# One more gate tile and eight key pages in the chain block; output weights with a second home in a decoder step

## The reference, cut to what matters

```python
oa, s_new, shift_new = rwkv_branch(za, shift0, s0, p)      # recurrent branch, a chain over the tokens
q, k, v, log_f = fox_features(zb, p['f_bias'], p['q_norm'], p['k_norm'])
ob = attend(q, k, v, log_f)                                 # samples: 16 pages of 128 keys and values each
merged = jax.nn.sigmoid(ga) * (oa @ p['proj_a']) + jax.nn.sigmoid(gb) * (ob @ p['proj_b'])
return (merged @ p['w_out']).astype(h.dtype), (k, v, log_f, s_new, shift_new)
```

## Time and profile before

| | |
|---|---|
| median of three runs | 859.84 us (859.52 to 865.72) |
| the profiled execution | 862.67 us, span 861.0 us |
| TensorE busy | 761.1 us, 88% of the span |
| VectorE, ScalarE, GpSimd busy | 382.5, 186.4, 145.3 us |
| mean granted TensorE clock | 0.942 |
| DMA | 220.26 MB, 256 GB/s over the span |
| chain that ended last, by engine | PE 17%, DMA 6%, DVE 1% of the span |

### The profile page before, as it was taken

How to read it: one execution, slowest core, us unless ns; L and a number is a source line. 1 busy time by engine, 2 the same in 40 slices (tenths; PEclk the granted TensorE clock), 3 DMA queues, 4 the chain that set the end, 5 groups by cost and what they waited for, 6 DMA issues and landing times. The chain is left out here.

```text
span 861.0 us, 20782 instructions
## 1 busy us (share of the span) xinstructions
PE 761.1 (88%) x8681; PEld 445.5 (52%) x8681; DVE 382.5 (44%) x722; ACT 186.4 (22%) x433; POOL 145.3 (17%) x294
## 2 busy tenths in 40 slices
PE   5999999998989999768898997889889987899985
PEld 2445666675666667624565664455644425444421
DVE  2222623228963174748666774633552222422213
ACT  2101321216332210031422320223111110111103
POOL 8500120007020020031504343422000000000000
PEclk9999999988999989768899998999989998999997
DMA  8721431211332113459899999988939999999993
GB/s 311 284 86 54 190 117 49 97 53 67 103 85 84 32 55 85 105 163 396 364 352 414 397 397 409 362 313 314 422 153 425 421 425 421 426 420 425 421 412 121
DMA packets 54647, 220.26 MB, mean 256 GB/s; under 512 B 21935, under 2 KB 24026, under 8 KB 30746
## 3 DMA queue, kind: packets, MB, share of 16 engines
q1 hardware_dynamic: 46576, 183.28, 54.5%
q0 software_dynamic: 7328, 35.48, 10.7%
q10 hardware_dynamic: 650, 0.18, 0.1%
HBM read 211.82 MB, written 7.09 MB: 254 GB/s over the span
## 5 line engine op out<-in xcount | busy, mean ns | idle before, releaser
L232 PE MATMUL bank<-arena 128*128 128x320 f32 x256 | 85.0, 469 | 3.1 <-DVEq L2200 1.8
L208 POOL DMA_DIRECT2D arena<-in_cv x116 | 59.9, 516 | 113.1 <-PE bank L1897 80.8
L513 PE MATMUL bank<-arena 128*128 128x512 f32 (+1 forms) x144 | 69.9, 624 | 1.4 <-DMA arena<-in_w_zb 1.4
L2508 PE MATMUL bank<-arena 128*32 128x512 f32 x512 | 65.4, 624 | 3.3 <-DMA arena<-in_w_exp 2.1
L2739 DVE TENSOR_TENSOR arena<-arena,bank 128x512 f32<-128x512 f32 x35 | 24.1, 687 | 97.2 <-PE bank L2478 94.2
L548 PE MATMUL bank<-arena 128*128 128x336 f32 x224 | 66.3, 450 | 0.6 <-ACT arena L429 0.6
L1590 DVE STREAM_TRANSPOSE arena<-arena 128x2048 f32<-128x2048 f32 x28 | 63.1, 2288 | 4.3 <-DMA arena<-in_ck 2.9
L232 PEld LDWEIGHTS bank<-arena 128*128 128x128 f32 x256 | 47.5, 199 | 24.8 <-issue 7.6
L1897 PE MATMUL bank<-arena 128*16 128x128 f32 x1024 | 35.6, 300 | 19.7 <-issue 11.4
L548 PEld LDWEIGHTS bank<-arena 128*128 128x128 f32 x224 | 41.5, 189 | 21.4 <-issue 1.7
L1389 ACT ACTIVATE arena<-bank 128x384 f32<-128x384 f32 (+6 forms) x63 | 25.1, 444 | 108.2 <-PE bank L232 31.9
(11 more groups left out here) (495 smaller groups left out, 1103.4 us busy)
## 6 DMA issues: line engine op xcount, KB each, us to landing
arena<-in_w_exp SPq DMA_DIRECT2D x95, 1024.0 KB, 19.1
arena<-in_ck SPq DMA_DIRECT2D x120, 256.0 KB, 6.6
arena<-in_cv POOLq DMA_DIRECT2D x116, 256.0 KB, 7.6
arena<-in_w_gate SPq DMA_DIRECT2D x8, 1024.0 KB, 4.8
arena<-in_w_za SPq DMA_DIRECT2D x7, 1024.0 KB, 6.9
arena<-in_w_zb SPq DMA_DIRECT2D x6, 1024.0 KB, 15.7
arena<-in_w_proj SPq DMA_DIRECT2D x8, 512.0 KB, 9.9
arena<-in_w_out SPq DMA_DIRECT2D x4, 1024.0 KB, 10.6
```

The lines of the kernel that those rows point to most:

```text
L208: eng.dma_start(tile[n:P:4, :], src[bass.ds(page, 1)].rearrange("a (p j) n -> (a p) (j n)", j=4))\
L232: mm = nc.tensor.matmul(bank[b][:, 0:TM], w[:, k, a, :], xnT[:, k, NMETA:T], start=(k == 0), stop=(k == KT - 1))
L513: mm = nc.tensor.matmul(bank[q % 6][0:n, :], xnT[:, k, i * P:i * P + n], w[:, k % 4, :], start=(k == 0), stop=(k == KT - 1))
L2508: mm = nc.tensor.matmul(bank[2][j * CAP:(j + 1) * CAP, :], xg[:, q % 2, k, j * CAP:(j + 1) * CAP], place[s][:, (k % 4) * 512:(k % 4 + 1) * ...
```

## The change

- `GT_PAIRS` is 15. Passes eight and nine of the chain get a quarter of tile 14 each; its other four matmuls lie among the output products, one behind the 2nd, 5th, 8th and 11th of twelve groups. Its copy follows on ScalarE, its store on SyncE. One tile is left to "cache". Output products use bank 4 in place of 3, the state's transposes bank 5.
- `cd` and `um` move in the arena behind `place[12]`, `xl` into `ar`, so that places 11 and 12 are free during the chain. SyncE loads key tiles 0 and 1 of sample 1 (eight pages, 2 MB) there, behind `rsuf` and ahead of the stores of tiles 12 to 14.
- In "cache" SyncE begins with key tile 2 of sample 1 (GpSimd keeps tile 3, now behind the gate stores), and it stores the state after the first projections. VectorE turns the first key tile before it waits for the variance, the second before the reciprocal.
- The gates are kept as two parts, prompt and samples; each gates load is two DMAs (8 runs of 1024 and of 256 bytes for each partition), and an `a` fill is two multiplies.
- `w_out[2]` is loaded twice: for the fills into `spare` (the prompt part of the gates) once the merge sum is complete, ahead of the keys of sample 7, and later into place 0 for the samples' output. `w_out[0]` and `[1]` come ahead of the keys of sample 6, `w_out[3]` ahead of the second copy of `[2]`.
- Fills are dealt 6, 2, 4, 5, 5, 5, 5 and none ahead of the weighing of sample 7.

```diff
-        GT_PRE, GT_LEVELS, GT_SOLVE, GT_SAMPLES, GT_PAIRS = 6, 9, 11, 12, 14
+        GT_PRE, GT_LEVELS, GT_SOLVE, GT_SAMPLES, GT_PAIRS = 6, 9, 11, 12, 15
...
+                for m in range(2):
+                    load_pages(sp, 11 + m, page_numbers(sp, m, 1), A["ck"])
                 gates_out(GT_SAMPLES, GT_PAIRS)
-                for i in range(2):
-                    sp.wait_ge(S(f"kept_gt{i}"), 16 * (GT_PAIRS // 2))
-                sp.wait_ge(S("w_sp_sb"), 1)
-                for g in range(NPAIR):
-                    sp.dma_start(O["rw_p"][2 * g:2 * g + 2]...).then_inc(S("kept_rw"), 16)
...
-                    if c < 7:
-                        chain_gate(c + 1)
+                    chain_gate(c + 1)
+
+                OUT_BANK = (0, 1, 2, 4)
                 pe.wait_ge(S("w_s"), NCH)
-                pe.wait_ge(S("w_gt_sb"), GT_PAIRS - GT_PRE)
+                pe.wait_ge(S("w_o1_sb"), 1)
...
+                        n = g * NT + j
+                        if n % 3 == 1:
+                            mm = gate_mm(pe, GT_PAIRS - 1, 3, (4 + n // 3,))
+                            if n // 3 == 3:
+                                mm.then_inc(S("w_gt"), 1)
+                pe.wait_ge(S("w_o1_sb"), 2)
...
-        fill_no = [0, 0, 5, 8, 11, 14, 18, 24, 28, len(kinds)]
+        fill_no = [0, 0, 6, 8, 12, 17, 22, 27, len(kinds), len(kinds)]
...
                 def gates_load(a):
-                    sp.dma_start(gates, gates_dram[a]).then_inc(S("gates_in"), 16)
-
-                for m in range(2):
-                    load_pages(sp, key_slot(1, m), page_numbers(sp, m, 1), A["ck"])
+                    sp.dma_start(gates, gates_dram[a, :, :, 0:SEQ]).then_inc(S("gates_in"), 16)
+                    sp.dma_start(gates_s, gates_dram[a, :, :, SEQ:TM]).then_inc(S("gates_in"), 16)
+
+                for n, page in enumerate(page_numbers(sp, 2, 1)):
+                    page_load(sp, place[key_slot(1, 2)], n, A["ck"], page, S("kept_key2"))
                 proj_load(sp, 0, 0)
                 proj_load(sp, 0, 1)
+                for g in range(NPAIR):
+                    sp.dma_start(O["rw_p"][2 * g:2 * g + 2]...).then_inc(S("kept_rw"), 16)
...
                 key_loads(5)
-                key_loads(6)
                 out_load(sp, 0)
                 out_load(sp, 1)
+                key_loads(6)
+                sp.wait_ge(S("m_ready"), ND)
+                sp.dma_start(spare, A["w_out"][2]).then_inc(S("spare_in"), 16)
                 key_loads(7)
                 sp.wait_ge(S("sco_ps"), DB - 1)
+                out_load(sp, 3)
                 out_load(sp, 2)
-                out_load(sp, 3)
...
-                for m in range(2, 4):
-                    pages = page_numbers(pool, m, 1)
-                    for n in range(4):
-                        page_load(nc.gpsimd, place[key_slot(1, m)], n, A["ck"], pages[n], S(f"kept_key{m}"))
+                pages = page_numbers(pool, 3, 1)
+                for i in range(2):
+                    pool.wait_ge(S(f"kept_gt{i}"), 16 * ((GT_PAIRS + 1 - i) // 2))
+                for n in range(4):
+                    page_load(nc.gpsimd, place[key_slot(1, 3)], n, A["ck"], pages[n], S("kept_key3"))
...
                 turn_bias(0)
+                turn_keys(1, 0)
                 dve.wait_ge(S("ov_ps"), 1)
                 TS(ovs, bank[7][:, 0:T], 1.0 / HD, GN_EPS, mult, add).then_inc(S("ov_ready"), 1)
-                turn_keys(1, 0)
+                turn_keys(1, 1)
                 dve.wait_ge(S("ort_ready"), 1)
                 nc.vector.reciprocal(ovs, ovs).then_inc(S("ov_rc"), 1)
-                turn_keys(1, 1)
```

More of the change, by code:

```diff
@@ L1446, in _ @@
                 gate_out(GT_SOLVE, 7)
-                for j in range(GT_SAMPLES, GT_PAIRS):
-                    gate_out(j, 3)
+                gate_out(GT_SAMPLES, 3)
+                gate_out(GT_SAMPLES + 1, 3)
                 act.wait_ge(S("w_or"), NCH)
@@ L1605, in out_load @@
             sp.dma_start(place[s], A["w_out"][c]).then_inc(full[s], 16)
-        gates = xnT.rearrange("p k t -> p (k t)")[:, 0:DM // P * TM].rearrange("p (d t) -> p d t", d=DM // P)
+        gates_all = xnT.rearrange("p k t -> p (k t)")[:, 0:DM // P * TM]
+        gates = gates_all[:, 0:SLOT].rearrange("p (d t) -> p d t", d=DM // P)
+        gates_s = gates_all[:, SLOT:].rearrange("p (d t) -> p d t", d=DM // P)
+        assert DM // P * SEQ == SLOT
+        spare = gates_all[:, 0:SLOT]
         valid = ident.rearrange("p (g c) -> p g c", g=NPAIR)[:, :, 0:2 * DS]
@@ L1683, in proj_fill, with out_full @@
             return full[proj_slot[2 * a + h]], 32 * (1 + (2 * a + h == 3))
+        out_tile = [place[out_slot[0]], place[out_slot[1]], spare, place[out_slot[3]]]
         def out_fill(c):
+            if c == 2:
+                return S("spare_in"), 16
+            return out_full(c)
+        def out_full(c):
             return full[out_slot[c]], (48, 16, kneed(6, 0) + 16, kneed(6, 1) + 16)[c]
@@ L2035, in _ @@
                 pe.wait_ge(S("sb_sb"), 1)
+                pe.wait_ge(*out_full(2))
                 for k in range(KT):
@@ L2238, in fill_out @@
                     if kind == "a":
-                        TT(mT[:, d, :], out[:, 0:TM], gates[:, d, :], mult).then_inc(S("fill_sb"), 1)
+                        ch(TT(mT[:, d, 0:SEQ], out[:, 0:SEQ], gates[:, d, :], mult))
+                        ch(TT(mT[:, d, SEQ:TM], out[:, SEQ:TM], gates_s[:, d, :], mult))
+                        dve.sem_inc(S("fill_sb"), 1)
                     else:
-                        ch(TT(btmp, out[:, 0:SEQ], gates[:, d, 0:SEQ], mult))
+                        ch(TT(btmp, out[:, 0:SEQ], gates[:, d, :], mult))
                         dve.sem_inc(S("fill_sb"), 1)
```

37 lines of the change are left out of this document (22 added, 15 removed).

## The result

| | median us | lowest to highest | runs |
|---|---|---|---|
| before | 862.78 | 859.52 to 867.46 | 4 |
| changed | 882.25 | 879.81 to 887.37 | 4 |

The ratio is 1.0245, 95% interval 1.0199 to 1.0291. The forecast was 849.2 us, faster, with 857 as the upper bound. The profiled execution of the changed kernel spans 878.2 us, 17.2 more than the 861.0 before.

A forecast was written before the change was run, and what follows sets the result against it. In the sample stage TensorE and DMA were both taken as close to full. +1.6 - 7.6 - 4.6 = -10.6 us took the profiled 861.0 to 850.4, 849.2 on the median's scale; range 842 to 857.

The forecast's parts named there:

- Part A: End of the chain block: with gate matmuls added there, it ends 1.6 us later, bounds -0.5 and +4.7.
- Part B: Opening of the sample stage: earlier key tiles and one gate tile bring sample 1's scores 7.6 us sooner, bounds -5 and -8.
- Part C, the wait for slot 7: Sample stage: TensorE's 3.24 us wait for slot 7's value pages goes, with the half clock behind it: -6.2 us.
- Part C, the new wait: First fills: VectorE waits for sample 1's exponentials, behind the first gates load and sigmoid: +4.2 us, bounds 0 and +5.
- Rival 2: Opening does not move: key tiles or the queue behind the state stores replace the removed wait; 853.8 us, chance 0.09.
- Part C, the other waits: Sample stage: old value-page waits go or shift, new ones come at samples 1 and 2: -3.1 us, bounds -9 and +2.
- Part C, the last iteration: End of the sample stage: without four fills, sample 7's weighing meets its last pages: +0.5 us, bounds 0 and +3.
- the two signs of being wrong: Sample stage: samples after the second take 25 us or more each, or the last weighing waits over 3 us.
- Rival 1: Sample stage: DMA becomes the pace of the samples, leaving a gain of 6 us, 854 us; chance 0.22.
- C: The stretch from sample 1's main scores to the last weighing, all its terms together: 4.6 us sooner.
- rival 3: Expert stage gives the gain back because its first weights are late: 858 to 860 us, chance 0.05.
- Rival 4: SyncE's queue waits for the merge sum before sample 7's keys; slower, near 869 us if complete at 529; chance 0.04.

The follow-up runs named there:

- e0_after: The changed kernel as it is, measured again in a later session: 1.0256 times before, median 18.0 us above before's.
- e4_half: The kernel before with each gates load split into two DMAs of equal width, 640 bytes per run: 1.0053 times before, median 869.83 us.
- e2_two: The kernel before with each gates load in two DMAs of four column blocks each, runs of 5120 bytes: 1.0021 times before, median 868.53 us.
- e10_splitkept: The changed kernel, load still split, with the gates load ahead of sample 2's last eight key pages and one fill ahead of the last weighing: 1.0037 times before.
- e9_tail: The changed kernel with a long-run gates load, ahead of sample 2's last eight key pages, and fills redealt, one ahead of the last weighing: 0.9949 times before.
- e9b_tail: The same kernel as e9_tail, measured once more in another session: 1.0005 times before, median 862.88 us.
- e7_front: The changed kernel with the gates load in one DMA of long runs, ahead of sample 2's last eight key pages: 1.0082 times before, median 866.90 us.
- e5_open: The changed kernel's first half alone (gate tile and eight key pages in the chain, order of the opening): 1.0077 times before, median 871.71 us.
- e6_deal: The changed kernel with the gates load in one DMA of long runs and the fills dealt as before: 1.0198 times before, median 879.53 us.
- e1_split: The kernel before with only each gates load split into runs of 1024 and 256 bytes: 1.0021 times before, median 868.57 us.
- h2_after: The changed kernel with GpSimd loading only half of each value page row for samples 1 to 7: 1.0034 times before, median 866.57 us.
- e3_fix: The changed kernel with gates stored in load order, so the load is one DMA of 10240-byte runs: 1.0141 times before, median 874.79 us.
- e13_dealonly: The changed kernel with nothing but the fills redealt, one ahead of the last weighing: 1.0170 times before, median 13.8 us above before's.
- e14_frontonly: The changed kernel with nothing but the gates load moved ahead of sample 2's last eight key pages: 1.0034 times before, median 7.9 us above before's.
- e8_openfront: The changed kernel's first half alone, with the gates load ahead of sample 2's last eight key pages: 0.9984 times before, median 863.34 us.

## Why the prediction was wrong

- **Part A: right within a microsecond, in part by luck.** The sample stage starts at 374.02 where 375.0 was forecast, but a second profile of the same kernel (e0_after) has 379.73. Better is the stretch from the first matmul of the last pass (353.67 in the earlier trace rows) to the stage: 19.8 us before (20.1 and 20.4 in e4_half and e2_two) and 21.1 now (21.6 in e0_after), 0.7 to 1.8 more, where +1.1 was forecast for it. The clock didn't stay at half: from 356 to 369 us it was 0.87 (0.50 in the earlier trace rows), and the gaps on "issue" are 3.6 us in all as before. Three of the four gate products among the outputs took 0.81 us each and the last, at half clock, 1.44: 3.9 us, where full clock would have been 2.2 by my price, but the outputs around them ran faster than before.
- **Part B: right.** Reciprocal ends at 387.3 (387.1), gate tile from 391.28 (390.9), main scores of sample 1 at 400.13 (399.6). The forecasts leave A out, and the stage started 0.55 us later, so B is -7.6 to the tenth. The scores start 26.1 us behind the stage's start where "within 26" was named.
- **Part C, the wait for slot 7: right on the wait, not on its worth.** It is gone. But the first merge product starts at 415.00, and by the terms of the sum it should have started at 411.3 (423.16, less 7.6, 3.24 and 1.0); 415.5 is where the third was wanted. The main scores took 5.78 us instead of 4.58 (granted clock 0.50 from 400 to 402 us and 0.72 to 404), and the weighing has a new gap of 1.67 us on "issue".
- **Part C, the new wait: the step that failed.** The term was +4.2, bounds 0 and +5; it measured 19.4, and 5.5 more at the second gates load. Place and mechanism were named rightly (sigmoid, exponentials behind it, two products ahead), and the 6.8 us from the sigmoid to the end of the exponentials held (430.61 to 437.42). Mis-sized was when the load is there: 412.6 by the prediction (406 + 6.6), 430.6 measured, 18.0 us late, which is the wait but for 1.4 us. Of these, 14.0 are the time from issue to landing: I took 6.6 us from the one-piece load (the 0.6 named for the small runs is not even in the 4.2), and the load took 20.6 from its issue. I priced the bytes of the 256-byte part and let the 1024-byte part pass as free, and did not price the surroundings: the load now runs beside the value pages of a weighing that starts earlier, in full engines. The other 4.0 are the issue, "about 406" and in fact 410.03: SyncE waits 7.1 us for the state stores that the change put ahead of the key pages. Rival 2 named that place in the queue and dismissed it, because the next item waits for scores anyway; but those scores were done at about 390.8 and the key pages left at 395.45. No run takes this wait away. By the bound of 512 bytes (the Trainium skill, DMA: Bandwidth & Descriptors, Specifications) the 1024-byte part counted as free. No run tests that bound by itself: the 1024-byte part landed after 14.6 us here and after 9.2 in e10_splitkept, where less ran beside it.
- **Part C, the other waits (-3.1): wrong in kind.** The waits for value pages between the scores of sample 2 and the last weighing (4.8 us) did go, and the new ones expected at samples 1 and 2 did not come: from the scores of sample 2 to those of sample 3 it took 20.6 us without any. Yet this stretch with the last weighing needs 164.5 us instead of 160.1, with one product fewer in it: 5.5 us stand at the second gates load and 5.4 in the last weighing.
- **Part C, the last iteration (+0.5, bounds 0 and +3): too low.** 5.4 us of waits and half the clock behind the last. I moved four products away from where they covered value pages and priced the cover at +0.5. With one product there e9_tail waits 3.8 us in the last weighing, e9b_tail 2.2. This is one of the two signs of being wrong that the prediction named (over 3 us) and that showed.
- **Rival 1 (DMA sets the pace): the mechanism was right, its price wrong.** I subtracted averages: 9.2 us to spare over 129. But from sample 1 to sample 2 there is little to spare before (share 0.92 from 407 to 436 us) and nothing once the opening has moved TensorE into just that stretch (1.01 in e7_front). Rival 1 should have said that the gain of B is lost there at once, as e5_open showed, and that the loss can exceed it, since everything behind a late load waits in turn.
- **The sum.** Between the main scores of sample 1 and the end of the last weighing the kernel lost 25.6 us where C said -4.6. Of the 30 us between, 15.2 are the first gates load, 5.5 the second and 4.9 the waits of the last weighing; the rest I have not traced. B held, so rival 2 did not come. The expert stage gave nothing back (263.4 us behind the last weighing, 264.8 before), so rival 3 did not come.
- **Rival 4** is real, but belongs to the old deal (e6_deal); in the changed kernel SyncE waits 1.8 us there.

No chance over 0.05 stood on "slower", because the one load whose shape the change altered had a bound taken from its old shape.

**Still open:** how much of SyncE's 12.7 us of issue time is the small runs and how much the full engines (5.3 us in e1_split, 5.2 in h2_after, 0.9 to 2.1 behind a load of long runs); what the wait for the state stores costs; and whether the kernel with all three mends beats the one before.

## What to carry to other kernels

Before changing the shape of a transfer, count its runs, and ask what runs beside it: at the same place in the queue, beside another queue's large packets, the last part of a load of 2048 small runs landed after 15.6 to 19.9 us (changed kernel) where one of long runs took 10.1 to 12.9 (e3_fix), though the bytes were the same. Time won ahead of a stretch in which DMA is full was mostly given back there; look at the share of that stretch, not at the stage's mean. And a load whose reader stands in front of other engines' work in a fixed order (here sigmoid, exponentials, sum, gate multiplication) passes its full lateness on to every one of them, so give it its place in the queue by who waits for it, and look at what the queue itself waits for ahead of it.

## What the runs showed of the hardware

- A small-run load also holds the engine that issues it. Behind the split load SyncE's next two DMAs took 12.70 us to issue, 12.72 in e0_after, 13.76 in e13_dealonly, 5.27 in e1_split and 4.60 in e4_half; behind loads of long runs 0.90 (before), 1.01 (e3_fix), 1.18 (e2_two, two DMAs) and at most 2.08 us (e6_deal). With the load early, its next eight key pages took 9.75 us (e10_splitkept) and 8.15 (e14_frontonly) behind small runs, 6.3 to 6.7 behind long ones (e7_front, e8_openfront, e9_tail, e9b_tail).
- The granted clock of one stretch differs between executions: behind the last weighing it was 0.93 in one profile (e9_tail) and 0.75 in another of the same kernel (e9b_tail), and the stretch took 4 us more. The same 32 matmuls took 7.09 us in the first and 9.81 in the second.
